# Half-split weights around the norms: from GpSimd to VectorE and ScalarE, and earlier in the queues

## What is computed

```python
def rmsnorm(x, g):
    x32 = x.astype(jnp.float32)
    y = x32 * lax.rsqrt(jnp.mean(x32 * x32, axis=-1, keepdims=True) + EPS)
    return y.astype(x.dtype) * g

def modulate(x, gain, shift, scale):
    return rms_norm(x, gain) * (1 + scale) + shift

for l in range(DEPTH):                      # first block
    xn = rmsnorm(x, norm_mix[l])
    ...
    x = x + y @ w_out[l]
    x = x + memory_cross_attention(rmsnorm(x, norm_cross[l]), mem_n, w_q_x[l], w_kv_x[l], w_o_x[l])
    x = x + swiglu(rmsnorm(x, norm_ffn[l]), w_gu[l], w_down[l])
return rmsnorm(x, final_norm)
```

## Time and profile before

| | |
|---|---|
| three runs | 3159.3, 3161.85 (median), 3199.03 us |
| the profiled execution | 3155.93 us |
| its span (first to last instruction) | 3153.6 us |
| its mean granted TensorE clock | 0.972 of full speed |
| TensorE busy | 2966.7 us, 94% of the span |
| VectorE, ScalarE, GpSimd busy | 1972.4, 1232.7, 261.1 us |
| weight subtractions on VectorE / GpSimd | 710 / 18 |

### The profile page before, as it was taken

One profiled execution on the slowest core, in us unless ns is written; L12 is line 12 of the kernel. 1 busy time (PEld: TensorE's weight loads), 2 busy tenths in 40 slices (PEclk: granted clock), 3 DMA queues, 4 the chain that ended last, 5 costly groups with the idle time before them and its releaser, 6 DMA issues.

```text
span 3153.6 us, 55499 instructions
## 1 busy us (share of the span) xinstructions
PE 2966.7 (94%) x23214; PEld 2790.6 (88%) x23214; DVE 1972.4 (63%) x3125; ACT 1232.7 (39%) x2095; POOL 261.1 (8%) x318
## 2 busy tenths in 40 slices
PE   8898989999898999999998889999999998999899
PEld 7788889878797998999876689999899998987899
DVE  5755688465567957767475556666566655435665
ACT  4454554344455444322344323222322223235443
POOL 1311000122101000000111120000100001000000
PEclk9999999899999999999999999999999998999899
DMA  6434467433355754555231114554255443242364
GB/s 199 123 107 148 134 207 244 161 119 101 116 167 167 244 200 140 181 171 178 81 122 40 54 54 148 167 167 141 94 161 163 155 138 107 85 144 90 125 194 140
DMA packets 245597, 447.66 MB, mean 142 GB/s; under 512 B 14483, under 2 KB 87076, under 8 KB 244580
## 3 DMA queue, kind: packets, MB, share of 16 engines
q1 hardware_dynamic: 239584, 430.79, 42.1%
q10 hardware_dynamic: 5764, 13.33, 1.3%
HBM read 443.01 MB, written 1.05 MB: 141 GB/s over the span
## 4 chain that ended last, share of the span: by engine, by line
PE 77%; DVE 12%; ACT 5%; issue 3%; POOL 1%; DMA 1%; ACTq 0%; DVEq 0%; SPq 0%; POOLq 0%
PE ps L1120 62%; DVE split L1817 3%; ACT split L1524 2%; PE ps L1148 2%; PE ps L1150 2%; DVE AR L1817 2%; PE ps L1149 2%; DVE A L1814 1%; DVE A L1869 1%; ACT A L1614 1%; DVE small L1985 1%; PE ps L1054 1%; ACT A L1532 1%; DVE X L1814 1%; PE ps L1362 1%
## 5 line engine op out<-in xcount | busy, mean ns | idle before, releaser
L1120 PE MATMUL ps<-AR,split 128*128 128x256 f32 x19392 | 2313.2, 280 | 34.9 <-DVE AR L1817 12.9
L1120 PEld LDWEIGHTS ps<-AR,split 128*128 128x128 f32 x19392 | 2253.0, 189 | 86.2 <-issue 44.2
L1817 DVE TENSOR_TENSOR split<-raw,split 128x1024 fp32r<-128x1024 f32 (+1 forms) x710 | 788.3, 1152 | 622.8 <-ACT split L1524 614.6
L1524 ACT ACTIVATE split<-raw 128x1024 fp32r<-128x1024 f32 (+2 forms) x728 | 682.4, 987 | 810.9 <-PE ps L1120 685.9
L2057 DVE SCALAR_TENSOR_TENSOR junk<-A,cb 128x1024 bf16<-128x1024 f32 x144 | 175.7, 1220 | 42.4 <-DMA A<-w_modT 40.2
L2057 DVE SCALAR_TENSOR_TENSOR A<-A,cb 128x1024 f32<-128x1024 f32 x144 | 175.4, 1218 | 0.0
L2293 POOL TENSOR_TENSOR A<-A 128x256 f32<-128x256 f32 (+1 forms) x45 | 40.7, 906 | 1581.9 <-ACT A L1532 1568.6
L1817 DVE TENSOR_TENSOR AR<-A,AR 128x256 fp32r<-128x256 f32 (+2 forms) x252 | 147.7, 586 | 24.7 <-ACT AR L1588 7.7
L1576 ACT ACTIVATE AR<-A 128x256 fp32r<-128x256 f32 (+1 forms) x132 | 68.4, 526 | 193.3 <-DVE A L1907 193.3
L1814 DVE SCALAR_TENSOR_TENSOR A<-A,ps 128x256 f32<-128x256 f32 (+1 forms) x196 | 95.2, 505 | 58.2 <-ACT A L1572 54.0
L1572 ACT ACTIVATE A<-ps 128x256 f32<-128x256 f32 (+1 forms) x132 | 63.3, 489 | 138.6 <-PE ps L1120 136.0
(11 more groups left out here) (231 smaller groups left out, 2290.7 us busy)
## 6 DMA issues: line engine op xcount, KB each, us to landing
A<-w_modT SPq DMA_DIRECT2D x144, 512.0 KB, 4.5
raw<-w_in SPq DMA_DIRECT2D x120, 512.0 KB, 4.5
raw<-w_gu SPq DMA_DIRECT2D x80, 512.0 KB, 4.7
raw<-ffn_a_in SPq DMA_DIRECT2D x80, 512.0 KB, 4.2
raw<-ffn_b_in SPq DMA_DIRECT2D x80, 512.0 KB, 4.2
raw<-ret_in SPq DMA_DIRECT2D x48, 512.0 KB, 4.1
raw<-w_down SPq DMA_DIRECT2D x44, 512.0 KB, 4.8
raw<-ffn_a_out SPq DMA_DIRECT2D x44, 512.0 KB, 4.3
```

The lines of the kernel that those rows point to most:

```text
L1120: mm = e.matmul(out[:, s:s + NT], wt[:, c, m_], xs(k0 + c, a + s, a + s + NT), start=first and part + s == 0, stop=last and part == 2 and ...
L1524: e.activation(hi, self.raw_view(q), ACT.Copy).then_inc(*self.mark(("w hi", q)))
L1817: return self.e.tensor_tensor(out, v, hi.bitcast(F32), ALU.subtract)
```

## The change

GpSimd no longer splits weights. `prepare` gets a flag `part`: with it, the block farthest ahead is taken with its first half only. The last block in front of a norm now calls `prepare(AHEAD, True)`, so that the first half of the block left out before is split within that last block. `prepare_beside` stands in front of `norm_sums` (in front of everything in `next_norm`), without GpSimd, so that the second half is split ahead of the root on ScalarE and ahead of the reciprocal on VectorE. Between the two blocks it moves from behind the latent sums to ahead of layer 1's final norm. In the cross attention a side generator `prepare_early(4, values)` lets four rounds of the pipeline go by, then finishes `values` and splits the block that the output projection's first `prepare` had split.

```diff
@@ project_t
             last = b0 + n == ncols and k0 + nk == c1
-            self.prepare(1 if hurry and last else AHEAD)
+            self.prepare(AHEAD, hurry and last)
@@ class Engine
-    def prepare(self, ahead, by="dve"):
+    def wanted(self, q, upto, part):
+        i, c0, _ = self.halves()[q]
+        return i < upto or i == upto and not (part and c0 > 0)
+
+    def prepare(self, ahead, part=False):
         upto = self.asked + ahead
         self.asked += 1
-        halves = self.halves()
-        while self.at_split < len(halves) and halves[self.at_split][0] <= upto:
-            self.split_half(self.at_split, by)
+        while self.at_split < len(self.halves()) and self.wanted(self.at_split, upto, part):
+            self.split_half(self.at_split)
             self.at_split += 1
@@
     def prepare_beside(self):
-        self.prepare(1, "pool")
+        self.prepare(1)
         self.asked -= 1
+
+    def prepare_early(self, rounds, before):
+        for _ in range(rounds):
+            yield
+        run(before)
+        self.prepare(AHEAD)
+        self.asked -= 1
+        yield
@@
     def next_norm(self, N, x, pair, beside=iter(()), **kw):
+        self.prepare_beside()
         self.some(beside, 6)
         self.norm_sums(N)
-        self.prepare_beside()
         self.some(beside, 4)
@@ layer_one
-        self.pipeline(units, values, 5)
-        run(values)
+        self.pipeline(units, values, 5, side=self.prepare_early(4, values))
@@ ret_part
-            self.prepare(1 if hd == 3 and b0 else AHEAD)
+            self.prepare(AHEAD, hd == 3 and b0 > 0)
@@ class VectorE
-    def split_half(self, q, by):
-        if by != "dve":
-            return
+    def split_half(self, q):
@@ class GpSimdE
-    def split_half(self, q, by):
-        if by == "pool":
-            i, c0, hi, lo = self.split_views(q)
-            self.e.wait_ge(*self.after(("w hi", q)))
-            self.e.tensor_tensor(lo, self.raw_view(q), hi.bitcast(F32), ALU.subtract).then_inc(*self.mark(("w lo", q)))
```

More of the change, by code:

```diff
@@ L2411, in prepare @@
                 self.at_load += 1
-            elif self.at_split < self.at_load and halves[self.at_split][0] <= upto:
+            elif self.at_split < self.at_load and self.wanted(self.at_split, upto, part):
                 self.at_split += 1
```

## The result

The changed kernel takes 3182.25 us (median of 20 runs, 3160.34 to 3206.43), the kernel before 3168.16 in 20 runs beside it (lowest 3153.06). The ratio is 1.0051, 95% interval 1.003 to 1.0072: slower by about 16 us, 9.5 to 23 (by the two medians 14.1). One of the 20 executions of the kernel before took 3416.77 us and does not count in the ratio. Run again in a later comparison (12 runs, 3187.64) the ratio was 1.0032 (1.0005 to 1.0059). Within 2% of no change, as forecast, on the forecast's side, and more than the +5.3 us that I had added up.

A forecast was written before the change was run, and what follows sets the result against it. TensorE, busy 94% of the span, was taken to bound the kernel. Feed-forward +5.2, mixing +0.2, wide +0.8, even -0.7, retention -0.4, cross +0.2 made +5.3 us, added to 3160.6: 3166, range 3147 to 3188.

The forecast's parts named there:

- The class and the sign: Whole kernel: within 2% of no change (chance 0.97), and slightly slower, by +5.3 us.
- The attention's split, the term 2.95: Cross attention: two early VectorE subtractions delay the last unit's scale, 2.95 us per layer, between 1.2 and 4.1.
- rival D: Norms: longer silences leave TensorE at 1.2 GHz for the next block, 100 us at 9 places, 3260; chance 0.02.
- The last square ends 11.4 us after the projection's start in either: Cross attention's output projection: earlier adds, then a half before the fifth add; last square's time unchanged at 11.4 us.
- The same term: Half split in the last block delays its adds: 0.8 us at four wide norms, 1.5 at mixing, hidden in long blocks.
- The half ahead of the root: Norms: reciprocal 2.3 us after last square; delays 0.8 feed-forward, 1.3 mixing, 0.6 wide or even, 0.9 retention.
- What comes back: Behind the norms: VectorE time no longer held by GpSimd shortens TensorE's waits, 12.3 us returned in all.
- Rival A: Norms: copies and subtractions hide beside TensorE's sums and last blocks, held time returns fully; -13 us, 3148; chance 0.20.
- C: All 18 subtractions: each worth the GpSimd-VectorE time difference, 20.6 us faster, 3140; chance 0.03.
- B: VectorE's queue: each subtraction before an add or reciprocal is paid, nothing returns; +17.6 us, 3178; chance 0.15.
- The upper bounds of the prediction: All delays at their largest (1.3 and 1.5 at every place, 4.1 twice), nothing returned: +32 us.

The follow-up runs named there:

- the second profile of before: The kernel before, unchanged, run and profiled again: ratio 0.9987 (0.9966 to 1.0007), span 3170.4 us.

## Why the prediction was right or wrong

**The class and the sign held**, 3182.25 lies within the range, and the forecast of 3166 is 16 us low. Two parts make that up: the kernel before itself ran 7.6 us above the 3160.6 I started from, and the medians lie 14.1 apart instead of 5.3. By the ratio the change cost +16 (9.5 to 23) in the first comparison and +10 (1.6 to 19) in the second. That 3182 fell inside the range is in part luck, since the pitch alone moves a run by more than the whole sum. The traces place 5.6 us at the norms. Against a profile of before whose clock did not fall behind the mixing norm's gap the change costs 4.5 more, 10. With a pitch worth 13 us a stretch, the runs do not say more.

**The attention's split, the term 2.95, was mis-sized: it is 4.4 in the changed kernel (7.2 or 7.3 less 2.8), above its upper bound of 4.1, and 3.7 alone.** The mechanism and the 3 us of delay were right (the last unit's scale ended at 392.0, forecast 391.5). I had left out what TensorE does behind the silence: its clock goes from 1.00 to 0.50, the unit's last 20 matmuls take 1.4 us more and half of the projection runs at half speed. This is rival D, at one place per layer and for some 3 us in all instead of 100. My argument against it, that the clock comes back soon behind the silences already there, did not hold, since at this place the clock had been up before the silence. The Trainium skill's rule, TensorE: Matmul & The Clock Gate, section What's actually happening, agrees with these rows (the slow state is the default and activity lifts it); I had applied it only to places where the clock was down anyway.

**"The last square ends 11.4 us after the projection's start in either" was the second failed step.** It is 13.6 us (410.76 less 397.21, and the same without the early split, 407.11 less 393.51; without the half in the last block the 2.3 to 2.5 us are gone). The first half waits until ScalarE has its copy done at 404.41, and VectorE's fifth add behind it: 2.2 us at the feed-forward norms, which I had at 0. The same term was right at most other places: 1.6 at the mixing norm (1.5), 0.9 at 512 tokens (0.8), none in the mixer's long last block; behind the retention, where I had it at 0, it is 0.8.

**The half ahead of the root held.** The reciprocal comes 2.12 us behind the last square (2.3), and the first chunk 0.58 (0.8), 1.44 (1.3), 0 to 0.8 (0.6) and 0.72 (0.9) us later.

**What comes back was somewhat more than forecast, and for another reason.** 2.3 in layer 0 as forecast, 0.5 in layer 1 (0), 1.7 on average at the wide norms (1.2), 2.0 behind the even mixer (1.3), 2.9 behind the retention (1.3); 5.3 at the mixing norm (2.6): 1.7 of gap, less than the 2.6 that I took, and 3.6 of clock, which I had not thought of on this side either and which is missing against the second profile of before. But it comes from moving work out from among the chunks. Rival A is out with that, and by its condition: the copies and subtractions did not hide. So is C: with VectorE doing every subtraction in the old place the ratio is 1.0005, where the quicker engine should have given 0.9935. The Trainium skill, GPSIMD Engine Reference, section 4.1 Engine selection, is right about the ratio of 2 (2.36 against 1.22 us), and the runs show no gain from it here. B stood for +17.6 with nothing returned; the runs are near it, but the traces show the returns. The upper bounds of the prediction add up to 31 and not 32, and the range's upper end lies 27 us above 3160.6, below both.

**Shown and not shown.** The early split's cost, the cost of each half, the worth of the held time and that the slow pitch comes without the change are shown by kernels that change one of them, in the traces; the ratios of these kernels overlap for the most part and do not order them. That the distance between the traces' 5.6 to 10 us and the runs' 16 is chance is argued from the interval alone.

## What to carry to other kernels

Before putting a piece of work "early", ask what stands behind it in each in-order queue, and price the delay at TensorE with its clock: a silence at a place where TensorE ran at 1.00 is paid once as idle time and often once more as slow matmuls behind it, and one that is shortened can give back both. Freeing one engine from another's shared time returned nothing here where the same work stayed among the chunks; only work done in front of them did. And where a bound engine runs long even rows of matmuls, compare two traces matmul by matmul before reading a difference of 1% as the change's.

## What the hardware did that was not expected

- Rows of equal matmuls (128x256, 128x128 weights) ran at one of two steady pitches, 113.3 or 117.8 ns, both at granted clock 1.00, for up to 3000 matmuls, in either kernel; 13.2 us for one 512-token feed-forward. Odd matmuls of 64 columns between pieces of such a row moved it through a cycle of slow, slow, fast.
- Behind the new silence of 3.21 us TensorE's granted clock read 0.50 up to 400 us and 0.62 in the 3 us after (1.00 before it); 48 matmuls took 8.16 us instead of 6.3.
- Behind one and the same gap of about 3 us (mixing norm) the clock fell to 0.50 or 0.60 in four profiles and stayed at 1.00 in one.
- An activation subtraction on VectorE that GpSimd had held to 1.12 and 2.01 us takes 0.43 without it; the two delays together are as long as the two weight subtractions on VectorE, so that with the two behind chunks 1 and 3 the exchange of engines changed nothing at that norm (0.03 us).
